# The swapped copy of each rotated head: four ScalarE copies in place of one TensorE product

## What is computed

```python
def rope_axis(x, cos, sin):
    x1, x2 = jnp.split(x, 2, axis=-1)
    return jnp.concatenate([x1 * cos - x2 * sin, x2 * cos + x1 * sin], axis=-1)

def apply_rope_2d(x, cos_r, sin_r, cos_c, sin_c):
    xr = rope_axis(x[..., :ROPE_AXIS_DIM], cos_r.astype(x.dtype), sin_r.astype(x.dtype))
    xc = rope_axis(x[..., ROPE_AXIS_DIM:], cos_c.astype(x.dtype), sin_c.astype(x.dtype))
    return jnp.concatenate([xr, xc], axis=-1)
```

## Time and profile before

| | |
|---|---|
| median of 3 runs | 2695.29 us (2692.04 to 2696.22) |
| the profiled execution | 2694.97 us, of which its span is 2693.3 us |
| PE busy | 2666.4 us, 99% of the span |
| DVE busy | 1723.9 us, 64% |
| ACT busy | 854.9 us, 32% |
| POOL busy | 101.3 us, 4% |
| mean granted TensorE clock | 0.997 of full |

### The profile page before, as it was taken

The page is one execution under the profiler, slowest core; times in us unless marked ns, Lnnn a source line. Parts: engine busy times, 40 slices in busy tenths (PEclk is TensorE's granted clock), DMA queues, the critical chain, the costliest instruction groups (busy, mean ns, idle before and its releaser), DMA issues.

```text
span 2693.3 us, 45871 instructions
## 1 busy us (share of the span) xinstructions
PE 2666.4 (99%) x17642; PEld 2586.8 (96%) x17642; DVE 1723.9 (64%) x2910; ACT 854.9 (32%) x1157; POOL 101.3 (4%) x193
## 2 busy tenths in 40 slices
PE   9999999999999999999999999999999999999998
PEld 5999999999999999999957999999999999999998
DVE  5898778686586877746675668677465554334345
ACT  4223422312443133124354431331232233223122
POOL 0000000000000000000000000000000000000000
PEclk9999999999999999999999999999999999999999
DMA  8443345353223443412101235444122222222212
GB/s 305 141 156 130 132 137 172 125 170 115 84 76 128 166 138 135 138 60 83 40 5 71 94 126 171 133 140 133 64 85 73 75 71 79 70 78 70 78 64 69
DMA packets 85746, 295.00 MB, mean 110 GB/s; under 512 B 10128, under 2 KB 13456, under 8 KB 85392
## 3 DMA queue, kind: packets, MB, share of 16 engines
q1 hardware_dynamic: 60160, 200.81, 22.0%
q0 software_dynamic: 25488, 92.81, 10.2%
HBM read 290.70 MB, written 2.88 MB: 109 GB/s over the span
## 4 chain that ended last, share of the span: by engine, by line
PE 94%; DVE 3%; ACT 1%; DMA 1%; issue 1%; DVEq 0%; ACTq 0%; SPq 0%
PE ps L463 44%; PE ps L464 44%; PE ps_x L658 1%; PE ps L634 1%; DVE w_lo L1147 1%; PE ps L773 1%; PE ps_sum L645 1%; DMA mix<-in_ada_head 1%; ACT w_hi L835 1%; PE ps_x L622 0%; PE ps L724 0%; PE ps_sum L613 0%; DVE g_lo L1161 0%; ACT tmp L960 0%; PE ps L517 0%
## 5 line engine op out<-in xcount | busy, mean ns | idle before, releaser
L1147 DVE TENSOR_TENSOR w_lo<-raw,w_hi 128x1024 fp32r<-128x1024 f32 (+2 forms) x360 | 430.4, 1196 | 665.1 <-ACT w_hi L835 662.4
L835 ACT ACTIVATE w_hi<-raw 128x1024 fp32r<-128x1024 f32 (+2 forms) x360 | 373.3, 1037 | 965.2 <-PE ps L464 958.3
L463 PE MATMUL ps<-h_hi,w_hi 128*128 128x320 f32 x1888 | 593.2, 314 | 0.7 <-DVE h_lo L1299 0.7
L464 PE MATMUL ps<-h_lo,w_hi 128*128 128x322 f32 x1888 | 587.1, 311 | 0.0
L463 PE MATMUL ps<-h_hi,w_lo 128*128 128x320 f32 x1888 | 586.7, 311 | 0.0
L464 PE MATMUL ps<-h_hi,w_lo 128*128 128x322 f32 x1888 | 586.2, 310 | 0.0
L464 PE MATMUL ps<-h_hi,w_hi 128*128 128x322 f32 x1888 | 585.2, 310 | 0.0
L463 PE MATMUL ps<-h_lo,w_hi 128*128 128x320 f32 x1888 | 584.3, 309 | 0.0
L1175 DVE CUSTOM_DVE_ANT_0 ps_x<-ada_w,cond 128x1024 f32<-128x1024 f32 x354 | 436.0, 1232 | 29.7 <-DVE tmp L1223 14.3
L464 PEld LDWEIGHTS ps<-h_hi,w_hi 128*128 128x128 f32 x1888 | 359.5, 190 | 2.6 <-issue 2.2
L463 PEld LDWEIGHTS ps<-h_hi,w_hi 128*128 128x128 f32 x1888 | 355.4, 188 | 3.7 <-issue 2.2
(11 more groups left out here) (158 smaller groups left out, 2904.7 us busy)
## 6 DMA issues: line engine op xcount, KB each, us to landing
raw<-in_weights SPq DMA_DIRECT2D x324, 512.0 KB, 3.3
ada_w<-in_ada_w POOLq DMA_DIRECT2D x177, 512.0 KB, 3.5
raw<-in_weights SPq DMA_DIRECT2D x32, 384.0 KB, 3.0
mix<-in_ada_head SPq DMA_DIRECT2D x16, 512.0 KB, 10.5
x<-in_x SPq DMA_DIRECT2D x8, 320.0 KB, 10.0
out_y<-mix SPq DMA_DIRECT2D x16, 160.0 KB, 1.9
mix<-in_spread SPq DMA_DIRECT2D x1, 1088.0 KB, 6.6
cond<-in_cond SPq DMA_DIRECT2D x1, 1024.0 KB, 13.6
```

The costliest lines, as they stand in the source:

```text
L463: pe.matmul(ps[:, 2 * slot, 0:TA], w[:, slot, ws], a(k)[:, 0:TA], start=begin, stop=end)
L464: mm = pe.matmul(ps[:, 2 * slot + 1, 0:width - TA], w[:, slot, ws], a(k)[:, TA:width], start=begin, stop=end)
L835: act.activation(w_hi[:, j % 2, 0:tiles * P], raw[:, j, 0:tiles * P], ACT.Copy).then_inc(w_hi_ready, 1)
L1147: dve.tensor_tensor(w_lo[:, j % 2, 0:tiles * P], raw[:, j, 0:tiles * P], w_hi[:, j % 2, 0:tiles * P].bitcast(F32), ALU.subtract).then_inc( ...
```

## The change

The product with the matrix `turn` goes, with the matrix itself, its load (so `CONSTS` falls from 5 to 4) and PE's waits for it. In its place ACT copies four blocks of 32 partitions from the head in SBUF to `ps_rot` in PSUM. The minus sign, which was in the matrix, moves into the table of sines. DVE's part is the same.

```diff
...
-            load_consts(((conv_w, "conv_w", consts_in), (turn, "turn", consts_in),
+            load_consts(((conv_w, "conv_w", consts_in), 
@@ -613,14 +613,6 @@
-                def head_turn(t):
-
-                    pe.wait_ge(head_normed, t + 1)
-                    if t:
-                        pe.wait_ge(head_ready, t)
-                    at = ROW_OF[t] * T
-                    pe.matmul(ps_rot, turn[:], mix[:, at:at + TS], start=True, stop=True).then_inc(head_turned, 1)
-
@@ -669,16 +661,14 @@
                     unit(t)
                     if 0 <= t - 1 < HEAD_ROWS:
                         head_sums(t - 1)
-                    if 0 <= t - 2 < HEAD_ROWS:
-                        head_turn(t - 2)
 
                 last = 4 * Q_QKV - 1
                 unit(last, stop_at=SCORES_AT)
                 pe.wait_ge(cache_in, 16)
+                pe.wait_ge(head_ready, K_AT + KVH)
                 pe.wait_ge(freed[0], 2 * (q0 + Q_QKV) + 1)
                 scores(0, 0, 0)
                 unit(last, begin_at=SCORES_AT, stop_at=TURN_AT)
-                head_turn(HEAD_ROWS - 1)
                 turn_v(0)
@@ -954,6 +944,17 @@
             def attention(q0):
+                def turn_head(t):
+
+                    act.wait_ge(head_normed, t + 1)
+                    if t:
+                        act.wait_ge(head_ready, t)
+                    at = ROW_OF[t] * T
+                    for part in range(0, P, ROT):
+                        other = part ^ ROT
+                        a = act.activation(ps_rot[part:part + ROT, :], mix[other:other + ROT, at:at + TS], ACT.Copy)
+                    a.then_inc(head_turned, 1)
+
@@ -989,6 +990,8 @@
                     if t < HEAD_ROWS:
                         act.wait_ge(row_ready, t + 1)
                         act.activation(tmp[:, t % 2, 0:T], kept, ACT.Square).then_inc(head_sq, 1)
+                    if 0 <= t - 1 < HEAD_ROWS:
+                        turn_head(t - 1)
@@ -1756,18 +1759,8 @@
-            out[at:at + axis // 2, 1] = np.sin(ang)
+            out[at:at + axis // 2, 1] = -np.sin(ang) if half == 0 else np.sin(ang)
```

More of the change, by code:

```diff
@@ L86 @@
 OUT_AHEAD = 4
+ROT = P // 4
 SCORES_AT, TURN_AT = 3, 5
@@ L97 @@
 H_BASE = [KD * n for n in range(2 * DEPTH)]
-CONSTS = 5
+CONSTS = 4
 CS, CP, CW = 1, TS + 3, T + 4
@@ L136, in build @@
         ident = sb("ident", [P, P])
-        turn = sb("turn", [P, P])
         mod = sb("mod", [P, DEPTH * ADA_T + 1, 2])
@@ L1830 @@
         "ident": np.eye(P, dtype=np.float32),
-        "turn": _turn(),
         "conv_w": _rows(a["conv_w"]).reshape(P, -1),
```

## The result

The changed kernel took 2700.92 us (2697.79 to 2705.09, 15 runs), the kernel before 2696.22 us in the same measurement (15 runs). The ratio is 1.0019, with a 95% interval of 1.0013 to 1.0026: some 5 us slower. The ratio lies just inside the 0.2% that I called the bound, and its interval reaches past it. The forecast was 2696.3 us, with 2690.5 to 2701.5 as the range.

A forecast was written before the change was run, and what follows sets the result against it. PE, 99% busy, was taken to bound the kernel; its 9.1 us saving would be taken back by a loop through ACT and DVE, leaving + 0.45 and + 0.5 us for the clock, about + 1.0: 2696.3 us, range 2690.5 to 2701.5.

The forecast's parts named there:

- The first case: The forecast itself: the loop through ACT and DVE takes back what PE saves, 2692 to 2700 us; chance 0.67.
- PE's saving: On PE, ten products gone at 0.86 us each, 8.6 us, plus some 0.5 us of waits: 9.1 us.
- the stage: Units leading into attention, from iteration 2's split on ACT to `row_max(0, 1)` on DVE: forecast to end 0.45 us later.
- The ring: Loop of ACT's split, DVE's normalisation, four copies, next split: 8.10 or 8.47 us for query heads, 12.33 for key heads.
- The price of the copies: On ACT, copies start 0.50 us apart: four delay the next instruction by 2.0 us, the last ending after 2.1 us.
- Fewer partitions aren't shorter: On ACT, a copy of 32 partitions by 512 columns costs as much as one of 128 partitions, about 0.6 us.
- Rival 2: Copies are short because they touch 32 partitions, with steps of 0.18 us: about 4.4 us faster, 2691 us; chance 0.11.
- rival 3: The loop through ACT and DVE never binds and the whole 9.1 us saving shows: 2686 us; chance 0.05.
- The slower rival: Each copy on ACT costs what the bias instruction costs, a step of 0.63 us: 2701 us; chance 0.17.
- PE's waits: PE waits for a head's square before its sums: 1.7 us after unit 7, 2 to 4 us after unit 8.
- The clock: PE's granted clock drops after the new waits; mostly hidden, the last may slow the scores: 0.5 us added.
- The signs: Expected in the changed profile: ten groups of four 0.6 us copies, splits right behind, PE waits, `row_max(0, 1)` near 1357.

The follow-up runs named there:

- Tiny and late copies: Changed kernel with copies of 8 columns instead of 512, placed behind the next iteration's split, rest of swapped copy left out: 2686.82 us, ratio 0.9971 to the kernel before.
- late place: Changed kernel with each head's copies behind the next iteration's split, the last head's excepted; there, with every copy made twice: 2703.58 us, ratio 1.0025 to the kernel before.
- late key heads: Changed kernel with only the two key heads' copies moved behind the next iteration's split: 2692.97 us, ratio 0.9986 to the kernel before.
- all copies late: Changed kernel with every head's copies but the last's moved behind the next iteration's split on ACT: 2688.83 us, ratio 0.9978 to the kernel before.

## Why the prediction was right, and what was off

- **The number**: inside the range, but only just, 0.6 us below its upper end. The first case, the forecast's own, was given 2692 to 2700 us, and 2700.92 lies above that. So the mechanism below was right, and its size too small.
- **PE's saving**, 9.1 us: right. Tiny and late copies show 8.97 us in the stage, and 0.9971 in the ratio.
- **The ring takes it back**: right, and shown from both sides. Opening it by order alone gives 10.5 us; lengthening it gives 23 us for 40 more copies, which in the late place cost 14.4.
- **The price of the copies**: a step of 0.50 us was forecast, 0.60 us measured (2.41 us for four, a single one 593 ns), with the next split at the end of the last copy and no overlap there either. The step was taken from two copies back to back on the same partitions; here each goes to another block. This is the term that was mis-sized. The rings were 8.51, 8.90 and 12.74 us where 8.10, 8.47 and 12.33 were forecast. From iteration 2 to iteration 10 that is 76.94 us against 73.83: 3.1 us of the 3.5 by which the stage's end missed. Of the other 0.4, 0.3 is the end of the last copies, which came 2.41 us after their start and not 2.1.
- **The estimate by the Trainium skill.** The Trainium skill (ScalarE: Activation LUTs, section What ACT_TABLE_LOAD costs) has about 93 ns of overlap back to back, and by my estimate from it the step was 0.52 us. That was a little nearer to the measured 0.60. On unchanged partitions the runs show an overlap of 0.09 us into SBUF and of 0.05 to 0.06 us into PSUM. From block to block the measurement decides: no overlap.
- **Fewer partitions aren't shorter**: right. 32 partitions by 512 columns took 593 ns, 128 by 512 took 598. Rival 2 had no ground, and rival 3 would have needed another order.
- **The slower rival** had a step of 0.63 us and 2701 us. The number came out at it, for another reason than the bias: its price was near, its cause wrong. That the two cases stand so close together makes the number a weak witness between them; the trace is what tells them apart.
- **PE's waits**: forecast 1.7 us after unit 7 and 2 to 4 us after unit 8, measured 3.28 and 2.22. The first is longer since the ring was 1.5 us later by then: from the split of iteration 2 to that of iteration 6 it took 1311.19 - 1272.53 = 38.66 us, where 37.20 were forecast.
- **The clock**: forecast 0.5 us. The clock fell after one of the two waits and stayed full after the other, and the ring set every split up to that of iteration 10 in any case. The third drop lies between that split and `row_max(0, 1)`, and it cost the stage nothing either: 1363.75 - 1349.47 = 14.28 us here, and 14.29 us in the kernel with late key heads, whose clock is full there. The two stretches, first of the change, then of late key heads:

```profile
1349.00:1364.00 15.00, 11.83 (x59) 9.03 (x57) 11.46 (x21) 10.16 (x17) 0.57 (x1) 0.89 0.01 2
...
1337.00:1352.00 15.00, 11.23 (x64) 8.88 (x62) 11.64 (x21) 9.97 (x17) 0.73 (x1) 1.00 0.01 2
```

- **The signs**: of those named as right, the order held, with the splits following the copies at once. `row_max(0, 1)` was to start within 1 us of 1357 and did not: it came at 1363.75, and 3.98 us late when both traces are counted from the split of iteration 2.
- **In sum**: the forecast difference was 1.0 us, of which the stage 0.45. The stage measured 3.98 us. With the 3.5 us for the step the forecast would have been some 4.5 us, and the ratio says 3.5 to 7.0.

## What to carry to other kernels

When work moves to an idle engine, its idle share says little; ask what each engine's next instruction for the bound engine stands behind, and add up the loop from that instruction back to itself. Put the moved work behind the instruction that feeds the bound engine, not ahead of it: here the same copies, one split later, turned 5 us of loss into 6 us of gain. Look for the longest wait that the moved work brings along (here a 4.15 us reciprocal, for two heads out of ten) as well as for its own length: in the change's place the wait, with the slow clock behind it, cost some 6 us with copies of 172 ns, and the full length 7 us more. And move all of the work that stands in the loop: one group of copies left in the old place kept a ring of 12.79 us.

## What the runs showed that was not expected

- ACT's back-to-back overlap of some 0.05 to 0.1 us is lost when the next instruction is on another block of partitions: four copies of 128 columns took 1.12 us against 0.87, four of 512 columns 2.41 us.
- A wait of 1.06 or 1.07 us behind unit 1 stands in all twelve traces. In eight of them a slow clock followed (granted 0.60 over 1260 to 1264 in the kernel before), in four none. In the kernel with all copies late the clock stayed full over the eight microseconds from 1260 on:

```profile
1260.00:1264.00 4.00, 3.32 (x25) 3.33 (x26) 2.02 (x3) 1.84 (x3) 0.00 (x0) 1.00 0.21 82
1264.00:1268.00 4.00, 4.00 (x29) 4.00 (x28) 0.82 (x3) 1.53 (x4) 0.00 (x0) 1.00 0.40 131
```

  So a drop can't be forecast from the length of that wait. It is worth some 1.5 us in that place (from the split of iteration 1 to that of iteration 2 it is 10.20 us before and 8.64 us here).
